# Rewriting the expert stage of a two-layer trunk: weight layout, prefetch, routing by token tile and an early row sum

## The reference, cut to what matters

```
def ec_moe(h, router_w, w1, w3, w2):                  # h (n, d), per segment
    cap = 2 * n // 16                                 # 32 tokens for each expert
    affinity = softmax(h @ router_w)                  # (n, 16)
    gate, idx = top_k(affinity.T, cap)                # each expert picks its tokens
    xg = h[idx]                                       # (16, 32, d)
    hid = silu(xg @ w1) * (xg @ w3)                   # w1, w3 (16, 1024, 1408)
    out = (hid @ w2) * gate                           # w2 (16, 1408, 1024)
    return zeros(n, d).at[idx].add(out)

def channel_sublayer(x, mod, ng, ...):
    h = rmsnorm(x, ng[2]) * (1 + mod[4]) + mod[3]
    return x + mod[5] * rmsnorm(ec_moe(h, ...), ng[3])
```

## Time and profile before

| | before |
|---|---|
| median of 3 runs | 3579.72 us (3577.03 to 3583.22) |
| the profiled execution | 3568.94 us, its span 3567.2 us |
| granted clock of TensorE, mean | 0.909 |
| PE / DVE / ACT / POOL busy | 74% / 25% / 15% / 8% of the span |
| moved by DMA | 676.24 MB, 553.6 MB of it expert weights |
| expert stage, layer 0 | about 1013 to 1802 us of the span |
| expert stage, layer 1 | about 2816 to 3567 us |

### The profile page before, as it was taken

How to read it: one execution, slowest core, us unless ns; L and a number is a source line. 1 busy time by engine, 2 the same in 40 slices (tenths; PEclk the granted TensorE clock), 3 DMA queues, 4 the chain that set the end, 5 groups by cost and what they waited for, 6 DMA issues and landing times. The chain is left out here.

```text
span 3567.2 us, 55702 instructions
## 1 busy us (share of the span) xinstructions
PE 2644.9 (74%) x23142; PEld 1365.3 (38%) x23142; DVE 888.8 (25%) x1895; ACT 523.7 (15%) x1076; POOL 299.6 (8%) x345
## 2 busy tenths in 40 slices
PE   4399966274958787777849577777778587777777
PEld 0144424142433222222324376777777322222222
DVE  1104015454021111111150055444445201000001
ACT  0100021321030000000020033332333100000000
POOL 0000000250010000000010222222222000000000
PEclk9899988696979999999979898888889799999999
DMA  9621100000218999999612300000000389999996
GB/s 383 260 73 71 71 0 1 0 1 24 83 66 329 414 413 414 414 403 414 255 40 71 116 12 12 12 12 12 12 12 3 119 342 413 413 413 411 404 409 255
DMA packets 180052, 676.24 MB, mean 190 GB/s; under 512 B 28568, under 2 KB 46784, under 8 KB 175344
## 3 DMA queue, kind: packets, MB, share of 16 engines
q1 hardware_dynamic: 178704, 672.45, 47.5%
q10 hardware_dynamic: 1120, 0.48, 0.0%
HBM read 666.35 MB, written 6.49 MB: 189 GB/s over the span
## 5 line engine op out<-in xcount | busy, mean ns | idle before, releaser
L1361 PE MATMUL bank<-moe_w,moe_xT 128*64 128x512 f32 (+3 forms) x3072 | 664.4, 570 | 223.8 <-DMA moe_w<-in_exp_w 221.6
L1361 PEld LDWEIGHTS bank<-moe_w,moe_xT 128*64 128x64 f32 (+1 forms) x3072 | 181.6, 124 | 711.0 <-DMA moe_w<-in_exp_w 378.2
L1381 PE MATMUL bank<-moe_w,moe_hidT 128*64 128x512 f32 (+1 forms) x1408 | 331.3, 628 | 15.1 <-ACT moe_hidT L1415 11.8
L1440 DVE TENSOR_TENSOR moe_silu<-bank,moe_silu 64x512 f32<-64x512 f32 (+3 forms) x96 | 56.6, 639 | 840.3 <-ACT moe_silu L1409 840.3
L1409 ACT ACTIVATE moe_silu<-bank 64x512 f32<-64x512 f32 (+3 forms) x96 | 46.2, 545 | 1218.0 <-PE bank L1361 1218.0
L1381 PEld LDWEIGHTS bank<-moe_w,moe_hidT 128*64 128x64 f32 (+1 forms) x1408 | 97.9, 128 | 223.9 <-issue 216.6
L391 PE MATMUL bank<-w_slab,mixT 128*128 128x512 f32 x384 | 166.2, 593 | 1.8 <-PE bank L391 1.5
L2048 PE MATMUL bank<-x_inv_and_t,p_prod 64*64 64x64 f32 x2560 | 154.1, 219 | 7.5 <-issue 6.6
L1454 DVE COPY moe_rows<-bank 32x512 f32 (+1 forms) x96 | 65.9, 686 | 356.0 <-PE bank L1381 355.1
L1810 DVE TENSOR_TENSOR x_inv_and_t<-bank,x_inv_and_t 128x512 f32<-128x512 f32 (+1 forms) x160 | 102.1, 638 | 194.3 <-PE bank L2048 193.6
L388 PE MATMUL bank<-mixT,w_slab 128*128 128x512 f32 x320 | 140.7, 601 | 12.2 <-DMA w_slab<-in_ab_w_in 11.1
(11 more groups left out here) (449 smaller groups left out, 3162.9 us busy)
## 6 DMA issues: line engine op xcount, KB each, us to landing
moe_w<-in_exp_w SPq DMA_DIRECT2D x512, 704.0 KB, 10.9
moe_w<-in_exp_w SPq DMA_DIRECT2D x352, 512.0 KB, 14.9
ada_slab<-in_ada_w SPq DMA_DIRECT2D x32, 1536.0 KB, 12.8
w_slab<-in_ab_w_in SPq DMA_DIRECT2D x11, 2048.0 KB, 7.4
wo_slab<-in_ab_w_out SPq DMA_DIRECT2D x16, 512.0 KB, 3.6
rw_slab<-in_rw_wk SPq DMA_DIRECT2D x4, 1024.0 KB, 6.6
rw_slab<-in_rw_wv SPq DMA_DIRECT2D x4, 1024.0 KB, 4.9
rw_slab<-in_rw_wr SPq DMA_DIRECT2D x4, 1024.0 KB, 4.8
```

Of the source, the lines that this page charges most:

```text
L1361: mm = pe.matmul(g.ps[k][64 * m:64 * m + M, 0:hi - lo], xg[:, j, c, :], wa[:, c % RA, m, lo:hi], start=(c == 0), stop=(c == DC - 1))
L1381: mm = pe.matmul(g.ps[5 + m][64 * m:64 * m + M, :], hidt[:, c, :], wb[:, c % RB, 512 * m:512 * m + 512], start=(c == 0), stop=(c == FC - 1))
```

## The change

All of it is in `stage_moe`; `stage_norm` and `Tail` are no longer called from there.

- **Weight layout.** Partition p takes rows 8p to 8p+7 of w1 and w3 (11p to 11p+10 of w2), no longer rows p, p+128, ... A DMA brings two row blocks of w1 or w3 (11 KB a row, 1.4 MB) or a group of four, four and three row blocks of w2 (16 and 12 KB a row). So the operands that meet the weights take every 8th column of `xn` and every 11th of `hid`.
- **Buffers.** Three slots of two row blocks for four pairs an expert (`PAIR_SLOT` 0, 1, 2, 0), two slots for three w2 groups (`GROUP_SLOT` 0, 1, 0). The stage starts with three pairs and two w2 groups issued, then the columns of shift and scale (`modc`).
- **Norm and routing by token tile**, in one block: square, root, scaling, turn and eviction (half by ACT, half by DVE) of each tile, and its logits with the router columns as the stationary operand, one turn for all logits. The rows are not turned back: the picks take the normed rows `xn`, and scale and shift are applied as DVE moves the picked rows to `xg`.
- **Picks.** All four quarters for the next four experts stand behind w1 and w3 of each fourth expert, three of them after the wait for the hidden rows; four banks. Put matrices are made during the first experts. All 16 experts are written out.
- **Row sum.** During the last four experts PE sums the rows of the first twelve into `acc` (`early`, kept by ACT), half a tile at a time, so that one matmul for each half tile is left. The norm at the end goes tile by tile: DVE adds, ACT squares and roots, POOL applies the gain, DVE adds to x.

```diff
-    RA, RB = 4, FC
+    PAIR_SLOT, PAIR_VISIT, VISITS = (0, 1, 2, 0), (1, 1, 1, 2), (2, 1, 1)
+    GROUP_SLOT, GROUP_VISIT, GVISITS, GROUP = (0, 1, 0), (1, 1, 2), (2, 1), ((0, 4), (4, 8), (8, FC))
...
-        wa = sb("moe_w13", [P, RA, 2, FF])
-        wb = sb("moe_w2", [P, RB, D])
-        hm = sb("moe_h", [P, NT, D])
+        wa = sb("moe_w13", [P, 3, 2, 2, FF])
+        wb = sb("moe_w2", [P, 2, 4, D])
+        xn = sb("moe_xn", [P, NT, D])
...
+        def pair_in(sp, e, c):
+            for k, w in enumerate((w1, w3)):
+                sp.dma_start(wa[:, PAIR_SLOT[c], k, :, :].rearrange("p r f -> p (r f)"),
+                             w[e].rearrange("(p c) f -> p (c f)", c=DC)[:, 2 * c * FF:2 * (c + 1) * FF]).then_inc(s_wa[PAIR_SLOT[c]], 16)
+
+        def group_in(sp, e, c):
+            lo, hi = GROUP[c]
+            sp.dma_start(wb[:, GROUP_SLOT[c], 0:hi - lo, :].rearrange("p r n -> p (r n)"),
+                         w2[e].rearrange("(p c) n -> p (c n)", c=FC)[:, lo * D:hi * D]).then_inc(s_wb[GROUP_SLOT[c]], 16)
...
             @block.sync
             def _(sp):
-                sp.dma_start(rw[:, :, :], a["router_w"][layer].rearrange("(c p) e -> p c e", p=P)).then_inc(s_rw, 16)
-                for c in range(RA):
-                    for k, w in enumerate((w1, w3)):
-                        sp.dma_start(wa[:, c, k, :], w[0, c * P:(c + 1) * P, :]).then_inc(s_wa[c], 16)
-
-        stage_norm(g, layer, 1, t0, ctx)
+                sp.wait_ge(s_rwz, 1)
+                sp.dma_start(rw[:, :, 0:NE], a["router_w"][layer].rearrange("(c p) e -> p c e", p=P)).then_inc(s_rw, 16)
+                for c in range(3):
+                    pair_in(sp, 0, c)
+                for c in range(2):
+                    group_in(sp, 0, c)
+                for s in segs:
+                    for k in range(2):
+                        sp.dma_start(modc[:, s, k, :], g.modp[layer, 1 - s:2 - s, (3 + k) * D:(4 + k) * D].rearrange("o (p c) -> p (o c)", c=DC)).then_inc(s_modc, 16)
...
+            @block.tensor
...
+                    for dc in range(DC):
+                        mm = pe.matmul(g.ps[4][32 * t:32 * t + 32, 0:P], rw[:, dc, :], hT[:, dc, t * P:(t + 1) * P], start=(dc == 0), stop=(dc == DC - 1))
...
+                dve.wait_ge(s_modc, 32 * ns)
+                for n, s in enumerate(segs):
+                    dve.wait_ge(s_bc, n + 1)
                     for j in range(2):
+                        dv.do(dve.tensor_scalar(sel[:, s, j, :], g.ps[n][:, :], tok[:, j:j + 1], None, ALU.is_equal))
...
+                def pair(e, c):
+                    if c == 3:
+                        sp.wait_ge(s_ua, 4 * e + 1)
+                    else:
+                        sp.wait_ge(s_ua, 4 * (e - 1) + (c + 1 if c else 4))
+                    pair_in(sp, e, c)
+
+                def group(e, c):
+                    if c == 2:
+                        sp.wait_ge(s_ub, 3 * e + 1)
+                    elif e:
+                        sp.wait_ge(s_ub, 3 * (e - 1) + 3 - c)
+                    group_in(sp, e, c)
+
+                for e in range(NE):
+                    if e:
+                        pair(e, 1)
+                        pair(e, 2)
+                    pair(e, 3)
+                    if e:
+                        group(e, 0)
+                        group(e, 1)
+                    if e + 1 < NE:
+                        pair(e + 1, 0)
+                    group(e, 2)
...
+                                mm = pe.matmul(g.ps[PICK_BANK[q]][:, (k * ns + n) * P:(k * ns + n + 1) * P], xn[:, 2 * s + j, c::DC],
+                                               sel[:, s, j, i * P:(i + 1) * P], start=(j == 0), stop=(j == 1))
...
+                def early(j, n):
+                    t, h = EARLY[j][n]
+                    pe.wait_ge(s_o, 4 * (NB - 1))
+                    pe.wait_ge(s_sto, len(PUT))
+                    if first_of[j] + n:
+                        pe.wait_ge(s_cmo, first_of[j] + n)
+                    for b in range(NB - 1):
+                        mm = pe.matmul(g.ps[7][:, :], selt[:, t // 2, b, (t % 2) * P:(t % 2 + 1) * P], oe[:, t // 2, b, 512 * h:512 * h + 512], start=(b == 0), stop=(b == NB - 2))
+                    mm.then_inc(s_cm, 1)
...
+                    for pr in range(4):
+                        sl = PAIR_SLOT[pr]
+                        pe.wait_ge(s_wa[sl], 32 * (VISITS[sl] * e + PAIR_VISIT[pr]))
...
                         mm.then_inc(s_ua, 1)
-
-                    pick(i + 1, j, 8 * (i + 1) + 2 * j)
+                    if j == 3 and i < NB - 1:
+                        if i == 0:
+                            pe.wait_ge(s_sto, min(3, len(PUT)))
+                        pick(i + 1, 0)
+                        pe.wait_ge(s_hid, e + 1)
+                        for q in range(1, 4):
+                            pick(i + 1, q)
+                    if i == NB - 1:
+                        early(j, 0)
                     pe.wait_ge(s_hid, e + 1)
...
                     for c in range(FC):
-                        mm = pe.transpose(g.ps[3 + c // 8][:, (c % 8) * M:(c % 8 + 1) * M], hid[:, c * P:(c + 1) * P], g.ident[0:M, 0:M])
+                        mm = pe.transpose(g.ps[3 + c // 8][:, (c % 8) * M:(c % 8 + 1) * M], hid[:, c::FC], g.ident[0:M, 0:M])
...
+                    for gr, (lo, hi) in enumerate(GROUP):
+                        sl = GROUP_SLOT[gr]
+                        pe.wait_ge(s_wb[sl], 16 * (GVISITS[sl] * e + GROUP_VISIT[gr]))
...
+                    if i == NB - 1 and len(EARLY[j]) > 1:
+                        early(j, 1)
...
+                for n, t in enumerate(range(t0, NT)):
                     for h in range(2):
+                        mm = pe.matmul(g.ps[2 * n + h][:, :], selt[:, t // 2, NB - 1, (t % 2) * P:(t % 2 + 1) * P], oe[:, t // 2, NB - 1, 512 * h:512 * h + 512], start=True, stop=True)
...
+                def sums(n):
...
+                        dve.tensor_tensor(half, g.ps[2 * n + h][:, :], half, ALU.add).then_inc(s_acc, 1)
+
+                def add(n):
...
+                    dve.scalar_tensor_tensor(g.x[:, t, :], acc[:, t, :], tssq[:, 2, t:t + 1], g.x[:, t, :], ALU.mult, ALU.add).then_inc(s_add, 1)
...
             @block.gpsimd
             def _(pool):
...
+                    pool.tensor_tensor(acc[:, t, :], acc[:, t, :], gain[:, 1 if t < 2 else 0, :], ALU.mult).then_inc(s_tg, 1)
```

494 lines of the change are left out of this document (248 added, 246 removed).

## The result

The changed kernel takes 3617.51 us (median of 4 runs, 3613.61 to 3622.84), the kernel before 3579.76 (4 runs, 3577.03 to 3583.22). The ratio is 1.0106, with a 95% interval of 1.0088 to 1.0123: **1.1% slower**, where 3490 was forecast. The profiled execution took 3622.84 us (span 3620.3), so it stands 53.1 us above the span of before, 3567.2.

The account below looks back on a forecast made before the run. The weight stream, 411 GB/s in both expert stages, was taken as the bound. Gains of 30.5 + 25.5 + 20.9 + 12.3 = 89.2 us gave 3479.7 for the profiled execution, 3490 for the median; range 3455 to 3545.

Parts of the forecast that it names:

- Step 1: Expert weight stream: longer rows move at 424 GB/s instead of 411, an expert's 17.30 MB in 40.8 us instead of 42.1.
- the rate stays 411: Rival on the expert weight stream: longer rows bring nothing, rate stays 411 GB/s, 3524 us in all; chance 0.17.
- Steps 2 to 5: Start of expert stages: 12.84 MB prefetch, wait for modulation columns to T0+35, expert 0 at T0+49.6 and T0+45.5, pipeline filling.
- step 5: Filling the pipeline at each stage's start: a DMA gap of about 20 us and a second short one, then none.
- Step 6: Steady expert loop: 15.0 us release path fits 16.7 us of transfer; stalls only after experts 3, 7, 11: 13.4 and 5.3 us.
- Step 7: Last expert: w2 ends at T0+711.1 in layer 0 and T0+702.3 in layer 1, gaining 30.5 and 20.9 us.
- step 4: Start of expert 0: PE starts at T0+49.6 in layer 0, picks taking 9.9 us, and at T0+45.5 in layer 1.
- Step 8: Early row sum and tiled norm at each expert stage's end: 25.5 us less in layer 0, 12.3 in layer 1.
- The sum: Whole kernel: the expert-stage gains add to 89.2 us, giving 3479.7 for the profiled execution and a forecast of 3490.
- Strided operands: Rival: strided stationary loads in picks and turns take twice as long, about 50 us in all, 3540; chance 0.12.
- The slower case: Rival: the expert loop becomes the bound, PE at half clock, 7.9 us more an expert, 3743 in all; chance 0.05.
- The list of what would show it: Trace signs by step, such as 424 GB/s inside stages; wrong if every expert has a stream gap or rate stays 411.

Follow-up runs that it names:

- e10: e9 with 80 semaphore increments on TensorE's queue behind its last matmul of layer 0's expert stage: 3448.95 us, ratio 0.9639 to the kernel before.
- e9: e5 with picks reading neighbouring columns and the modulation columns loaded ahead of the expert weights: 3478.78 us, ratio 0.9722 to the kernel before.
- e1: Kernel after, picks and turns reading 128 neighbouring (wrong) columns: 3559.1 us, where the kernel before, run beside it, took 3585.4.
- e2: Kernel after plus 8 idle matmuls while TensorE waits for silu, in nine experts: span 3591.3 us, kernel after 3620.3.
- e5: Kernel after with picks spread one quarter an expert and w2 loaded and released in six groups, two rows at a time: span 3519.2 us.
- e8: Kernel before with 128 semaphore increments on TensorE's queue ahead of the layer-1 RWKV stage: that stage, from its first matmul, 1016.7 us, before 1004.1.
- e4: Kernel after with spread picks, one of two expert matmuls left out for all but first and last column chunks: span 3538.0 us.

## Why the prediction was wrong, by its steps

**Step 1, row length: right, but not realised.** With a queue that doesn't run dry the rate is 420 to 424 in the full slices (e10 above), and two silus of e9 stand 40.84 us apart, the 40.8 of the forecast:

```profile
1245.02 1.45 ACT L1480 ACTIVATE moe_silu<-bank 64x512 f32<-64x512 f32 x3 [23.00 <-PE bank L1419]
1285.86 1.45 ACT L1480 ACTIVATE moe_silu<-bank 64x512 f32<-64x512 f32 x3 [36.29 <-PE bank L1419]
```

So the rival "the rate stays 411" was wrong, and the Trainium skill's flat rate from 512 B on ("DMA: Bandwidth & Descriptors", Specifications) does not tell the 3% between rows of 4 to 5.6 KB and rows of 8 to 11 KB. Whether it is the row or the size of a transfer I did not separate; 8 KB rows in w2 were enough.

**Steps 2 to 5: right but for the picks.** Modulation columns at T0+35.3 (forecast 35). Expert 0 began at T0+55.6, forecast 49.6; the 6 us are the picks, 15.53 for 9.9. In layer 1 T0+44.4, forecast 45.5: there the picks' 7.89 us are near the 8.2 of the sum by luck, since the sum had plain loads at half clock and the trace has strided ones. The two gaps of step 5 are there as well. GB/s from 1019 to 1099 us, in slices of 2 us:

```profile
GB/s 83 282 411 428 434 439 417 434 425 422 417 445 459 410 410 442 114 1 0 0 0 0 0 0 0 0 0 0 0 0 65 315 434 428 208 0 0 51 248 439
```

The prefetch ends in the slice from 1051 (T0+33.4 = 1052.5), nothing moves for some 26 us (forecast about 20), and a second short gap begins at 1089.

**Step 6 failed, and with it 59.7 us in layer 0 and 34.6 in layer 1** (silu to silu 686.1 against 626.4, 654.9 against 620.3). Two terms. The long intervals: 34.6 us over ordinary ones in layer 0, forecast 14.4; 14.9 in layer 1, forecast 8.3. Here the mechanism was right and the size off: 6.15 us of added picks were 11.7 with the stride (three of four quarters at 3.9), and without the stride (e1) an interval of this kind is 2.5 us over the ordinary ones, not 11.5. The ordinary intervals: "it just fits, with 1.7 us to spare". It did not fit: 43.4 and 42.7 us for 40.8, over 15 intervals 39.5 us in layer 0 and 28.0 in layer 1. The path that I had at 15.0 us is, in expert 8, 4.95 (pair 3) + 2.50 (the wait for silu) + 1.55 (turns) + 0.47 + 5.1 (the first group; 1466.86 to SP's issue at 1471.92) + 2.2 (what a load takes beyond its bytes, taken over from the sum) = 16.8, against 16.7 of transfer. All of the spare was used, 1.6 us of it by the slower first group and 0.4 between w13 and w2, where the turns were longer by 0.7. A sum that leaves 1.7 us on 16.7 can't carry the word "none elsewhere". But this sum was not the whole path either: without the stride in the turns (e1) an ordinary interval was still 43.1, with a first group 1.4 us shorter (e2) still as long as in after, and in e9 it was 40.8 with the turns at 1.55 as here. The next w13 pairs wait in turn for pair 0's use, behind a late third group, which my step 5 worked out once for the start and step 6 left out. What closed the gap was the earlier release at both places (e5), and in layer 0 the plain picks besides (e9).

**Step 7** follows: w2 of the last expert ended at 1798.75 = T0+779.6 in layer 0, forecast T0+711.1, of which 6.0 are step 4, 59.7 the intervals from silu to silu, and 2.8 the rest; 3603.77 = T0+737.2 in layer 1, forecast T0+702.3.

**Step 8: right.** From the last w2 matmul to the last add:

```profile
1794.63 4.12 PE L1442 MATMUL bank<-moe_w,moe_hidT 128*64 128x512 f32 x12 [2.93 <-DMA moe_w<-in_exp_w]
1816.72 3.34 POOL L1554 TENSOR_TENSOR moe_xn<-moe_xn,moe_w 128x1024 f32<-128x1024 f32 x1 [0.25 <-ACT moe_w L1490]
1820.16 1.28 DVE L1541 SCALAR_TENSOR_TENSOR x_res<-moe_xn,moe_tail_norm,x_res 128x1024 f32<-128x1024 f32 x1 [2.23 <-POOL moe_xn L1554]
```

22.7 us for 21 in layer 0 and 16.5 for 15.6 in layer 1, against the 46.5 and 27.9 worked out from the earlier trace rows. POOL's 3.34 us a tile (2.5 in the sum) are the difference.

**The sum** took untouched stages at nothing. The RWKV stage cost 30.6 us, a third of the forecast gain. The 5.7 us up to layer 0's stage stay open: that time lay between 1014.0 and 1019.2 us in all 17 other profiled executions but carries no order by what was changed, and e8, the kernel before with padding behind that point, has 1018.2 too, so before's 1013.4 is the low end of a scatter or of a placement, not the change's doing.

**The rivals.** Strided operands, at 0.12, is what happened at the picks. Its price was about right, 50 us for the 57.7 of e1, and by its own sum it would have given 3540 alone. The slower case, at 0.05, had the right quantity and the right place, the interval of each expert, and its turning point was right as well: the gain of 89.2 us is gone once 32 intervals are 2.8 us longer than the sum has them, and they were, on average, 4.0 us longer in layer 0 (59.7 over 15) and 2.3 in layer 1 (34.6). But I let only half clock throughout lead there, and so gave it a far price and a small chance. It came by small terms together, a path at least 1.8 us longer and lumps nearly twice as long, which make the expert stages 16.7 us slower by the two profiled executions; the untouched stage adds 30.6.

**The list of what would show it** named the case: "wrong it is if the stream has a gap in every expert".

## What to carry to other kernels

Larger transfers in the same buffer space are also coarser releases: before you cost a longer row, follow each slot from its last reader to the first byte of its next load, with everything that the issuing queue holds behind it, and want a spare of several us, not of one tenth. A weight layout that puts a stride into a stationary operand moves its cost to every load of it, and small loads belong ahead of a prefetch. When a run leaves work out to see whether an engine is the bound, look in its trace whether the engine was less busy before you read the time. When a change alters the number of instructions ahead of a loop, time the loop as well, and try a shift before you blame or praise the change.

## What the runs showed of the hardware

- A stationary operand of 128 columns of float32 loads in 192 ns when they are neighbours and in 335 ns with a step of 8; with a step of 11 and 64 rows, 218 for 138 ns.
- The HBM stream of one core moved 420 to 424 GB/s in the full slices of e10, in rows of 8 and 11 KB (the last of w2 4 KB), and 411 over 647 us of before, in rows of 4 and 5.6 KB, both at a full queue.
- The same stage took 1002 to 1035 us depending on how many instructions stood ahead of it on TensorE's queue, and 256 more brought it back within 3.4 us, at a scatter of 4; a semaphore increment on that queue took 0.16 us (64 in 10.2, 128 in 19.9).
- Two matmuls that write different sets of 64 partitions ran side by side: with one of them left out, a pair of row blocks took the same 4.94 us (e4).
- At the start of the w2 matmuls TensorE's granted clock stood at its lower level in the experts of after that I read, behind the 2.5 us pause for silu (0.50 from 1140 to 1145) and also behind a lump of strided picks without one (0.66 from 1425 to 1430). Eight idle matmuls in the pause kept it at 1.00 (e2), and the silu-to-silu time did not move (686.1 and 686.2).
